# Masks on VectorE, two chunks issued early, low halves in two pieces: one change to the mixer and delta-rule stages

## What is computed

```python
h = rmsnorm(x, norm1_w)
u, q, k, v, z, a, bt, xr, gr = split(h @ w_in)        # mixer panels
y_pool = pool_mixer(u, ...)                            # 4 tiles of 128 columns
y_gdn  = gated_deltanet(q, k, v, z, a, bt, ...)        # 6 heads, 6 tiles
y_lru  = rglru_mixer(xr, gr, ...)                      # gated recurrence, 6 tiles
x = x + concat(y_pool, y_gdn, y_lru) @ w_out
x = x + conv_ffn(rmsnorm(x, norm2_w), ...)
# in gated_deltanet, for each head and chunk:
q, k, v = silu(causal_dwconv(qkv, 4 taps)); q, k = l2norm(q), l2norm(k)
m = strict_lower(beta * (k @ k.T) * decay) + eye       # its inverse is applied
wu = triangular_solve(m, [k * beta * exp(g), v * beta])
```

## Time and profile before

| | us |
|---|---|
| median of 3 runs (lowest, highest) | 2154.99 (2154.62, 2155.24) |
| the profiled execution | 2154.94 |
| its span | 2153.1 |
| TensorE busy | 2131.6 (99%) |
| VectorE busy | 1350.1 (63%) |
| ScalarE busy | 972.4 (45%) |
| GpSimd busy | 166.2 (8%) |
| mean granted TensorE clock | 0.996 |

### The profile page before, as it was taken

The page is one execution under the profiler, slowest core; times in us unless marked ns, Lnnn a source line. Parts: engine busy times, 40 slices in busy tenths (PEclk is TensorE's granted clock), DMA queues, the critical chain, the costliest instruction groups (busy, mean ns, idle before and its releaser), DMA issues.

```text
span 2153.1 us, 29306 instructions
## 1 busy us (share of the span) xinstructions
PE 2131.6 (99%) x11771; PEld 1858.2 (86%) x11771; DVE 1350.1 (63%) x1431; ACT 972.4 (45%) x1017; POOL 166.2 (8%) x140
## 2 busy tenths in 40 slices
PE   9999999999999999999999899999999999999998
PEld 8888888888888888888888888888888888888887
DVE  4666566556666666567788654776546765467655
ACT  5444445444444445444666334445433443333433
POOL 0000000000120100020000700002200021000310
PEclk9999999999999999999999999999999999999999
DMA  8755555666666556655554025556555565556553
GB/s 248 232 178 177 176 172 177 197 183 186 186 176 189 169 173 216 210 156 174 176 159 159 35 79 194 197 180 194 193 196 191 181 195 195 194 177 195 193 191 125
DMA packets 341424, 386.19 MB, mean 179 GB/s; under 512 B 26090, under 2 KB 287675, under 8 KB 341051
## 3 DMA queue, kind: packets, MB, share of 16 engines
q1 hardware_dynamic: 319979, 372.35, 54.0%
q10 hardware_dynamic: 21328, 12.14, 2.3%
HBM read 382.36 MB, written 4.00 MB: 179 GB/s over the span
## 4 chain that ended last, share of the span: by engine, by line
PE 95%; DVE 2%; ACT 1%; POOL 0%; issue 0%; DMA 0%; SPq 0%; DVEq 0%; POOLq 0%; ACTq 0%
PE acc L1512 42%; PE acc L1522 22%; PE acc L1567 7%; PE acc L1568 7%; PE acc L1572 7%; PE aux L1688 1%; PE aux L1666 1%; PE aux L1835 1%; PE acc L1627 1%; PE aux L1875 1%; PE aux L1677 1%; PE aux L1600 1%; DVE w_lo L815 1%; ACT w_hi L391 1%; POOL proj L1459 0%
## 5 line engine op out<-in xcount | busy, mean ns | idle before, releaser
L815 DVE TENSOR_TENSOR w_lo<-raw,w_hi 128x2048 fp32r<-128x2048 f32 x346 | 803.6, 2322 | 523.5 <-ACT w_hi L391 523.3
L391 ACT ACTIVATE w_hi<-raw 128x2048 fp32r<-128x2048 f32 x346 | 662.5, 1915 | 643.4 <-PE acc L1522 348.4
L1512 PE MATMUL acc<-act_x,w_hi 128*128 128x512 f32 x2496 | 607.6, 395 | 2.0 <-ACT w_hi L391 1.1
L1512 PEld LDWEIGHTS acc<-act_x,w_hi 128*128 128x128 f32 x2496 | 462.6, 189 | 94.9 <-DVE act_x L927 1.3
L1512 PE MATMUL acc<-ff_x,w_hi 128*128 128x512 f32 x1536 | 366.6, 391 | 0.0
L1522 PEld LDWEIGHTS acc<-act_x,w_lo 128*128 128x128 f32 x2496 | 319.8, 191 | 12.0
L1512 PEld LDWEIGHTS acc<-ff_x,w_hi 128*128 128x128 f32 x1536 | 282.4, 188 | 54.7
L1522 PE MATMUL acc<-act_x,w_lo 128*128 128x256 f32 x2496 | 324.4, 283 | 0.0
L1522 PEld LDWEIGHTS acc<-ff_x,w_lo 128*128 128x128 f32 x1536 | 196.9, 191 | 7.5
L1522 PE MATMUL acc<-ff_x,w_lo 128*128 128x256 f32 x1536 | 199.4, 283 | 0.0
L1567 PE MATMUL acc<-w_hi,act_x 128*128 128x512 f32 x464 | 180.8, 390 | 0.0
(11 more groups left out here) (281 smaller groups left out, 1636.1 us busy)
## 6 DMA issues: line engine op xcount, KB each, us to landing
raw<-in_ffn_up SPq DMA_DIRECT2D x96, 1024.0 KB, 5.2
raw<-in_w_in_c SPq DMA_DIRECT2D x64, 1024.0 KB, 5.7
raw<-in_w_in_ab SPq DMA_DIRECT2D x52, 1024.0 KB, 5.0
raw<-in_ffn_down SPq DMA_DIRECT2D x48, 1024.0 KB, 5.0
raw<-in_w_in SPq DMA_DIRECT2D x40, 1024.0 KB, 5.3
raw<-in_w_out_ab SPq DMA_DIRECT2D x16, 1024.0 KB, 5.1
raw<-in_w_out_c SPq DMA_DIRECT2D x16, 1024.0 KB, 5.2
raw<-in_w_out SPq DMA_DIRECT2D x16, 1024.0 KB, 5.0
```

Source lines behind the costliest of these rows:

```text
L391: copy = lambda out, in_, **k: nc.scalar.activation(out, in_, ACT.Copy, **k)
L815: tt(w_lo[:, c % 2], raw[:, c], w_hi[:, c % 2].bitcast(F32), ALU.subtract).then_inc(lo_ready, 1)
L1512: mm(out(j), wide(w_hi[:, c % 2])[:, k, j * P:(j + 1) * P], x[:, 8 * r + k, :, :].rearrange("p a s -> p (a s)"), start=(r == 0 and k == 0) ...
```

## The change

It makes five edits. SyncE issues chunks 0 and 1 of the second layer's second out-projection panel before it waits for the gated outputs, and chunks 2 and 3 before the constants. ScalarE, in the first mixer panel, rounds chunk 3 before it waits for `resid_normed` and empties the bank's half after that. The fourth convolution of the queries runs one chunk earlier on ScalarE and VectorE, its group's Silu and square follow one chunk earlier, and the recurrent gate product of VectorE one chunk later. In `middle()` GpSimd keeps the first level of groups 0 and 1 and the second level of group 0; VectorE makes the first level of group 2 and the second level of groups 1 and 2, ahead of the last panel's evacuation. The low halves are written in two pieces, the pool's inside round 0 and the recurrence's inside round 1, each between the updates of the transposed inverse and the copies back; the out-projection's parts wait for one piece each.

```diff
 # SyncE
-            def load(gp, dst, src):
-                for c in range(4):
+            def load(gp, dst, src, chunks=range(4)):
+                for c in chunks:
                     sp.wait_ge(lo_ready, 4 * gp - 3 + c)
...
             load_down(AT_OUT_C, a["w_out_c"], 0)
+            load_down(AT_OUT_C + 1, a["w_out_c"], PANEL, chunks=(0, 1))
             sp.wait_ge(gated, 8)
             sp.dma_start(lnf, row_of(a["ln_f"], D)).then_inc(lnf_landed, 16)
+            load_down(AT_OUT_C + 1, a["w_out_c"], PANEL, chunks=(2, 3))
             load_middle()
-            for i in range(1, N_OUT):
+            for i in range(2, N_OUT):
 # ScalarE
                 for c in range(4):
-                    if c % 2 == 1:
+                    if c % 2 == 1 and not (late and c == 1):
                         low_to(gp, c // 2, out(c // 2))
                     if c < 2:
                         split(gp, c + 2)
                     else:
                         split(gp + 1, c - 2)
+                    if late and c == 1:
+                        act.wait_ge(resid_normed, 1)
+                        low_to(gp, 0, out(0))
...
-                    act.wait_ge(resid_normed, 1)
...
-                n = 4 * p + c - 20
-                if 0 <= n < 18:
+                at = 4 * p + c
+                for n in (2, 3) if at == 22 else (at - 20,) if 20 <= at < 38 and at != 23 else ():
...
-                if p >= 6 and c == 0:
-                    x = p - 6
+                if at in (23, 28, 32, 36):
+                    x = (23, 28, 32, 36).index(at)
 # VectorE
-                if (p, c) == (5, 2):
+                if (p, c) == (5, 3):
                     dve.wait_ge(lru_gelu, 1)
                     tt(m2, xc, gr, ALU.mult).then_inc(lru_y, 1)
...
-                if 20 <= at < 38:
+                if 20 <= at < 38 and at != 23:
                     conv_qkv(at - 20)
+                if at == 22:
+                    conv_qkv(3)
...
+                def mask(g, level, done):
+                    tt(four(gBm, g), four(gB, g), const(level).unsqueeze(1).broadcast_to([P, 4, P]), ALU.mult
+                       ).then_inc(done, 1)
...
                 first_inverse(1)
+                dve.wait_ge(gram_masked, GDN_H)
+                mask(2, M_LEVEL, level_first)
+                dve.wait_ge(x_init, 2)
+                mask(1, M_LEVEL + 1, by_vector)
+                first_inverse(2)
+                dve.wait_ge(x_init, 3)
+                mask(2, M_LEVEL + 1, by_vector)
                 dve.wait_ge(w_used, 4 * AT_OUT2)
                 to_tile(4 * IN2_PANELS[N_IN2 - 1], 1, N_AB + N_C + N_IN2 - 1)
-                first_inverse(2)
-                dve.wait_ge(x_init, 3)
-                tt(four(gBm, 2), four(gB, 2), const(M_LEVEL + 1).unsqueeze(1).broadcast_to([P, 4, P]), ALU.mult
-                   ).then_inc(last_masked, 1)
                 split(AT_OUT2, 1)
...
-                better(0)
+                def low_of(y, first, n):
+                    tt(act_lo[:, first:first + n, :], y, act_hi[:, first:first + n, :].bitcast(F32), ALU.subtract
+                       ).then_inc(mid_split, 1)
+
                 dve.wait_ge(mid_hi, 1)
-                for y, first, n in ((tiles(U0, POOL_G), 0, POOL_G), (tiles(XR0, LRU_B), POOL_G + GDN_H, LRU_B)):
-                    ins = tt(act_lo[:, first:first + n, :], y, act_hi[:, first:first + n, :].bitcast(F32), ALU.subtract)
-                ins.then_inc(mid_split, 1)
-                with dve.Fori(1, 5) as r:
+                better(0, amid=lambda: low_of(tiles(U0, POOL_G), 0, POOL_G))
+                better(1, amid=lambda: low_of(tiles(XR0, LRU_B), POOL_G + GDN_H, LRU_B))
+                with dve.Fori(2, 5) as r:
                     better(r)
 # GpSimd
             first_level(0)
             first_level(1)
-            second_level(0)
-            first_level(2)
-            second_level(1)
+            pool.wait_ge(x_init, 1)
+            level(0, const(M_LEVEL + 1)).then_inc(level_masked, 1)
 # TensorE
                 if part == 0:
-                    pe.wait_ge(mid_split, 1)
+                    pe.wait_ge(mid_split, c + 1)
...
-                pe.wait_ge(level_masked, 2)
+                pe.wait_ge(by_vector, 1)
                 first_product(1)
                 pe.wait_ge(x_copied, 3)
-                pe.wait_ge(last_masked, 1)
+                pe.wait_ge(by_vector, 2)
                 first_product(2)
...
-                        pe.wait_ge(level_masked, 3 * r + g)
+                        pe.wait_ge(level_masked, 3 * r + g - 1)
```

More of the change, by code:

```diff
@@ L182, in program @@
             sem(n) for n in ("decay_in", "decay_cum", "decay_arg", "decay_exp", "gram_ready", "gram_masked"))
-        level_open, level_first, level_masked, last_masked, x_init, x_turned, x_copied, x_next, w1_ready, w1_out, z_ready_inv = (
-            sem(n) for n in ("level_open", "level_first", "level_masked", "last_masked", "x_init", "x_turned", "x_copied",
+        level_open, level_first, level_masked, by_vector, x_init, x_turned, x_copied, x_next, w1_ready, w1_out, z_ready_inv = (
+            sem(n) for n in ("level_open", "level_first", "level_masked", "by_vector", "x_init", "x_turned", "x_copied",
                              "x_next", "w1_ready", "w1_out", "z_ready_inv"))
@@ L297, in load_up, with load_down @@
                 load(gp, lambda c: wide(raw[:, c]), up_piece(w, col))
-            def load_down(gp, w, col, row0=0):
+            def load_down(gp, w, col, row0=0, chunks=range(4)):
                 load(gp, lambda c: raw[:, c], lambda c: w[bass.ds(row0 + c * 512, 512), bass.ds(col, PANEL)
-                                                         ].rearrange("(k p) n -> p k n", p=P))
+                                                         ].rearrange("(k p) n -> p k n", p=P), chunks)
             def outs(w, gp0):
@@ L402, in low_to, with panel @@
                 copy(out, halves(h)[:, :, 1, :]).then_inc(low_copied, 1)
-            def panel(gp, out, between=None):
+            def panel(gp, out, between=None, late=False):
                 for c in range(4):
-                    if c % 2 == 1:
+                    if c % 2 == 1 and not (late and c == 1):
                         low_to(gp, c // 2, out(c // 2))
@@ L797, in _ @@
             for p in range(N_IN2):
-                panel(AT_IN2 + p, tile_pair(4 * IN2_PANELS[p]), lambda c: mixers(p, c))
+                panel(AT_IN2 + p, tile_pair(4 * IN2_PANELS[p]), lambda c: mixers(p, c), late=p == 0)
             middle()
@@ L1205, in middle, with better @@
                 first_inverse(1)
+                dve.wait_ge(gram_masked, GDN_H)
[5 more added lines that the diff above has]
+                mask(2, M_LEVEL + 1, by_vector)
                 dve.wait_ge(w_used, 4 * AT_OUT2)
                 to_tile(4 * IN2_PANELS[N_IN2 - 1], 1, N_AB + N_C + N_IN2 - 1)
-                first_inverse(2)
-                dve.wait_ge(x_init, 3)
-                tt(four(gBm, 2), four(gB, 2), const(M_LEVEL + 1).unsqueeze(1).broadcast_to([P, 4, P]), ALU.mult
-                   ).then_inc(last_masked, 1)
                 split(AT_OUT2, 1)
-                def better(r, last=False):
+                def better(r, last=False, amid=None):
                     for g in range(3):
@@ L1217, in better @@
                         tt(four(gXT, g), four(gXT, g), bank4(aux[:, g, :]), ALU.subtract).then_inc(x_next, 1)
+                    if amid:
+                        amid()
                     if not last:
```

3 lines of the change are left out of this document (removed).

## The result

The changed kernel takes 2143.38 us, median of four executions (2141.07 to 2143.61), against 2155.11 (2154.62 to 2156.21, four executions) for the kernel before on the same chip. The ratio is 0.994, with a 95% interval of 0.9927 to 0.9952. That is 11.7 us by the medians. The forecast was 2141.5, a gain of 13.4; the measured time is 1.9 us above it, inside the range of 2139.5 to 2146 but above the 2140.3 to 2142.8 of the forecast's own case. The profiled execution took 2143.49 us (span 2141.7), 11.45 less than the profiled one of before.

What follows compares the result with a forecast made beforehand. TensorE, busy 95% of the span, was taken as the bound. 1.7 + 1.0 + 2.9 + 5.0 + 4.0 - 1.2 = 13.4 us off 2154.94 gave 2141.5 us, range 2139.5 to 2146.

Steps and rivals of the forecast that it cites:

- the forecast's own case: Whole kernel: all five terms come, at most 2.5 us of new stalls; 2140.3 to 2142.8 us, chance 0.68.
- The sum over TensorE: Whole kernel: TensorE's waits that go, plus slow stretches going with them, less new waits; 13.4 us gained.
- Early chunks: Second layer's second out-projection panel: TensorE's wait goes as chunks 0 and 1 load early; 1.7 us, or 0.
- High half: First mixer panel: converting chunk 3 ahead of the wait for the scalings removes TensorE's wait; 1.0 us.
- Query convolution: First sums of squares: wait of 1.3 and slow stretch of 1.6 both go; 2.9 us, 1.3 if it stays.
- Masks: Delta-rule stage: waits of 1.37 and 3.15 shrink to 0.6 and 0.2, slow stretch goes; 5.0 us.
- Low halves: First two inverse rounds: two pieces remove the wait and the slow clock behind it; 4.0 us.
- what takes their place: Inverse rounds: GpSimd late at first round's third group (0 to 1.3) and next round (0 to 1.2); 1.2 us booked.
- Rival A: Delta stage: VectorE's masks shut GpSimd out, first product waits 4.8 us; 2145.8 us, chance 0.09.
- Rival B: Delta stage or 16 one-column products at 1087.87: clock still falls, 1.4 to 1.6 each; 2143.0 or 2144.5, chance 0.17.
- Rivals C and D: C: clock stays low in the delta stage, 2161, chance 0.02; D: waits move on, 2151 to 2155, chance 0.04.

Runs made afterwards that it cites:

- e6: Changed kernel with all chunks of the second layer's second out-projection panel loaded behind gain vector and constants, as before: 2144.87 us, ratio 0.9943.
- e12: The kernel before, no edit, one more execution with a profile: 2155.84 us.
- e5: Changed kernel with the fourth query convolution, its Silu and square, and the gate product back in their old chunks: 2146.01 us, ratio 0.9949.
- e11: Changed kernel with the query convolution back and both one-column groups (16 and 24 products) 32 columns wide: 2144.76 us, ratio 0.9945.
- e3: Changed kernel with both low halves again back to back on VectorE between first and second round: 2144.77 us, ratio 0.995.
- e8: Changed kernel with the 24 head-square sums 32 columns wide and VectorE's out-projection split moved behind the last round: 2140.86 us, ratio 0.9926.
- e7: Changed kernel with ScalarE waiting again for the scaled residual ahead of chunk 3's high half: 2142.65 us, ratio 0.9935.
- e2: Changed kernel with the 24 products over the heads' squares 32 columns wide instead of one: 2141.65 us, ratio 0.9936.
- e10: Changed kernel, no edit, one single execution with a profile: 2143.73 us.

## Why the prediction was near, and where it failed

**What bounds.** The sum over TensorE was the right frame. T - w agrees within 0.04 us over four executions, and each edit undone gave back a sum of waits and slow stretches that its timeline shows. Undone one by one the five terms give 15.5 us (3.69 + 1.07 + 2.92 + 5.57 + 2.26), not 13.8: slow stretches come and go between the profiles.

**Early chunks, 1.7.** Measured 1.60 between the profiles. Undone, 3.7 in the profiled execution, 1.1 to 2.2 in the others. The step took the wait of one execution (1.77) for the wait of the place; e6 and e12 have 2.23, and a fall behind it. A size, not the mechanism.

**High half, 1.0.** Measured 1.09, undone 1.07. Right.

**Query convolution, 2.9.** Measured 2.89, undone 2.92 (e5) and 2.85 (e11). The choice to take the slow stretch as gone was right. It was luck in one sense: e12 shows an execution of the kernel before that has no fall there.

**Masks, 5.0.** Measured 5.17, undone 5.57, of which 2.95 are waits and 2.6 a longer slow stretch. What is late next was named with its sizes: 0.6 against 0.54, 0.2 against 0.16.

**Low halves, 4.0, less 1.2 for what takes their place.** Measured 1.44 + 1.63 = 3.07, against 2.8. Undone it is 2.26, since no slow stretch came with the wait (e3); that the booked 1.6 fits is in part the luck of the execution read. The new wait is at the third group of the first round, as named, 0.87 long inside the 0 to 1.3; the second piece costs nothing. e8 shows its cause, the split beside the masks, which the text had listed among the things that run there.

The Trainium skill ("SBUF — State Buffer", section "Who interferes with whom") says that a VectorE instruction with two SBUF inputs contends with a GpSimd instruction that reads SBUF, and calls the port pair that they share an exclusive lock. The traces agree that GpSimd is held up: 12 masks take 5.02 us alone and 7.51 beside 3.43 us of low halves, and 6.09 beside the piece of 1.75. That is 73% and 61% of VectorE's time, and for the split of e8 2.4 of 2.54 us.

**Rival A**, GpSimd shut out of the first group: the first product waits 2.05 us, not 4.8. VectorE's masks leave GpSimd turns between them. It fell.

**Rival B**, the clock still falls, priced at 1.4 to 1.6 each and 2143.0 for one. This is the time that came by both medians, 2143.1 to 2143.4, but at a place that B didn't name; three of the eleven executions came at 2141.0 to 2141.2, within 0.5 us of the forecast itself. Both of its places ran at 1.00. The failed step is the sentence "Outside these places the edits touch nothing". Each edit moved no work there, and yet the sums at 1246 had a fall behind them in all four profiles of the changed kernel, and had none in both of the kernel before. That term was missing: -1.6. The prediction looked for falls only behind waits, as the slow stretches of the earlier trace rows all stood behind waits, while this one follows a string of one-column products with no wait over 0.56 us ahead.

**Rivals C and D** had no part: no stretch of low clock in the 128-column work from 1193 to 1244, and the waits didn't move on.

**The numbers.** Of the 2.0 us between the forecast (2141.5) and the profiled execution (2143.49), the missing term is +1.6, the start of the kernel +0.86, and the terms of the sum were 0.4 too small together (13.8 for 13.4). 1.6 + 0.86 - 0.4 = 2.1, less the 0.09 between 7 and 843 us. That the range held the result owes something to its having been drawn around rival B, whose price for one fall fits though its place doesn't.

**What stays open.** It isn't known why the same 24 narrow products are followed by a fall in eight of nine profiles of the changed kernel and its narrow variants, and not in e7 or in the two profiles of the kernel before. With 32 columns no fall followed in three of three. The runs didn't vary the time at which the sums start with all else fixed, so whether it is that, or what ran in the microseconds ahead, isn't settled. Nor is it shown what the three times near 2141.1 of the changed kernel held, or why the first loads start slowly for a time that differs.

## What to carry to other kernels

When TensorE is the chain from end to end, add up its waits place by place, name what is late next at each, and book a slow stretch behind a wait as likely, 1.6 us here, and not as sure: read two executions before taking one for the kernel. Look for short products too: a string of one-column products behind which the clock falls can be made 32 columns wide, which cost nothing here (2.76 us for the 24 loads both ways). And take the time of the first weight loads off both profiles before comparing them, since it alone differed by up to 1.2 us.

## What the runs showed of the hardware

- The same first 32 weight loads took from 5.27 us (e2) to 6.43 us (e10), and the rest of the changed kernel agreed within 0.04 us over four executions. The Trainium skill ("TensorE: Matmul & The Clock Gate", section "What's actually happening") says that the number of slow products at the start changes from run to run; the traces agree, with these numbers.
- The clock fell from 1.00 to 0.50 with no wait over 0.56 us ahead, behind 24 one-column products, and cost 1.59 us.
- Waits don't decide a fall by their length alone: 3.08 us had none behind it (e3), 1.26 us had one (e5, e11), and 1.26 at the same place had none in e12. Over the 14 profiles, ten of 13 waits of 1.26 to 3.15 us at four places had a fall behind them (the adjoining 1.37 and 3.15 of the masks counted once), and none of the 14 waits of 2.05 or 2.06 at the first product.
- GpSimd got turns between VectorE's instructions: its first group of masks wasn't late beside two VectorE masks back to back (first product's wait 2.05, as before). It lost 61 to 73% of the time of the low halves beside it, and 2.4 us to one long split of 2.54.
